# A gated mixture kept in SBUF between the attention blocks and the output blocks of two layers, with its row loads issued by ScalarE

## The reference

```python
# layer 0 (_even_mixer, branch), for latent and context rows
gate = jax.nn.silu(p[..., o_kv:])
return (jnp.concatenate([conv, attn], axis=-1) * gate) @ w_out
# layer 1 (_odd_mixer, branch), for latent rows
return (attn * jax.nn.silu(p[..., o_v:])) @ w_out
# after each layer
x = _post_norm(x, gate[:, None, :] * y, ln_g[layer], ln_b[layer])
```

## Time and profile before

| | |
|---|---|
| median of 3 runs | 4097.86 us (4092.61 to 4101.16) |
| the profiled execution, its own time | 4095.32 us |
| its span in the profile | 4093.6 us |
| PE busy | 3785.0 us, 92% of the span |
| DVE, ACT, POOL busy | 35%, 16%, 14% |
| mean granted TensorE clock | 0.975 of full speed |
| last `att_a_` product ends, first `out_a_` product starts | 1142.90 and 1182.55 us |
| last `att_c_` product ends, first `out_c_` product starts | 1830.87 and 1858.49 us |

### The profile page before, as it was taken

How to read it: one execution, slowest core, us unless ns; L and a number is a source line. 1 busy time by engine, 2 the same in 40 slices (tenths; PEclk the granted TensorE clock), 3 DMA queues, 4 the chain that set the end, 5 groups by cost and what they waited for, 6 DMA issues and landing times. The chain is left out here.

```text
span 4093.6 us, 59155 instructions
## 1 busy us (share of the span) xinstructions
PE 3785.0 (92%) x24989; PEld 1899.2 (46%) x24989; DVE 1423.6 (35%) x2623; ACT 652.7 (16%) x1339; POOL 593.2 (14%) x868
## 2 busy tenths in 40 slices
PE   8899997899979999988999999898998888888998
PEld 1354443334534444544444444453446666664443
DVE  0499983332322214222100013344534333331411
ACT  0100001122211000321110000143432222221000
POOL 0011011120100001110000011342103232322100
PEclk9899998999989999999999999999999999999999
DMA  8788996882265456436555478537773333334663
GB/s 291 293 293 288 333 358 211 297 304 81 92 249 174 165 185 228 133 122 228 182 166 172 152 288 299 202 114 246 269 240 105 111 107 118 103 101 153 222 220 103
DMA packets 360949, 818.39 MB, mean 200 GB/s; under 512 B 27922, under 2 KB 63786, under 8 KB 352994
## 3 DMA queue, kind: packets, MB, share of 16 engines
q1 hardware_dynamic: 257424, 472.27, 34.4%
q0 software_dynamic: 75008, 284.12, 19.3%
q10 hardware_dynamic: 28256, 58.26, 3.8%
HBM read 695.86 MB, written 118.70 MB: 199 GB/s over the span
## 5 line engine op out<-in xcount | busy, mean ns | idle before, releaser
L1135 PE MATMUL gemm_a_g_ps<-store_w,turned 128*128 128x512 f32 (+1 forms) x1152 | 454.8, 557 | 2.4 <-PEq L205 2.4
L1135 PE MATMUL out_c_g_ps<-store_w,turned 128*128 128x512 f32 (+1 forms) x1024 | 399.3, 553 | 0.0
L839 DVE SCALAR_TENSOR_TENSOR pmods_acc<-pmods_w,cond,pmods_acc 128x512 f32<-128x512 f32 x540 | 384.4, 749 | 24.7 <-issue 1.3
L1135 PEld LDWEIGHTS gemm_a_g_ps<-store_w,turned 128*128 128x128 f32 x1152 | 208.6, 190 | 248.1 <-issue 248.1
L2410 PE MATMUL scan_g_ps<-store_w,turned 64*64 64x512 f32 x2048 | 291.8, 607 | 10.4 <-DVE outlet_stage L2424 4.7
L1135 PEld LDWEIGHTS out_c_g_ps<-store_w,turned 128*128 128x128 f32 x1024 | 184.6, 190 | 213.7 <-issue 213.7
L1135 PE MATMUL att_a_g_ps<-store_w,turned 128*128 128x512 f32 x512 | 240.2, 600 | 6.6 <-ACT outlet_stage L2182 3.9
L1135 PE MATMUL out_a_g_ps<-store_w,turned 128*128 128x512 f32 x512 | 222.4, 597 | 1.1 <-PEq L205 1.1
L1135 PE MATMUL gemm_hq_g_ps<-store_w,turned 128*128 128x512 f32 x512 | 220.0, 592 | 1.7 <-DVEq L3230 1.7
L1135 PE MATMUL out_a_g_ps<-store_w,turned_c 128*128 128x512 f32 x512 | 220.2, 592 | 0.0
L1135 PE MATMUL feat_g_ps<-store_w,turned 128*128 128x512 f32 x384 | 179.9, 618 | 11.7 <-ACT outlet_stage L1761 9.6
(11 more groups left out here) (447 smaller groups left out, 4941.9 us busy)
## 6 DMA issues: line engine op xcount, KB each, us to landing
store_w<-in_w_in SPq DMA_DIRECT2D x160, 1024.0 KB, 5.5
pmods_w<-in_w_mod POOLq DMA_DIRECT2D x40, 2048.0 KB, 11.7
store_w<-in_a_w_in SPq DMA_DIRECT2D x48, 1024.0 KB, 9.4
store_w<-in_c_w_in SPq DMA_DIRECT2D x48, 1024.0 KB, 5.2
mods_w<-in_w_mod SPq DMA_DIRECT2D x32, 1024.0 KB, 9.3
store_w<-in_a_w_out SPq DMA_DIRECT2D x32, 1024.0 KB, 5.0
scan_raw<-s_feat SPq DMA_DIRECT2D x112, 256.0 KB, 4.6
s_feat<-feat_o POOLq DMA_DIRECT2D x16, 1536.0 KB, 7.8
```

The lines of the kernel that those rows point to most:

```text
L839: v.scalar_tensor_tensor(a, src, x, a, ALU.mult, ALU.add)
L1135: mm = pe.matmul(to, lhs, self.store.slot[i % self.store.NS][:, k, :width], start=first, stop=last)
```

## The change

- `rows_t`, a tile of 128 x 4 x 2048 float32, lives in SBUF from `att_a_` to the end of `out_c_`. The scaled attention results go straight into it; `ost` and its stores are gone. POOL loads the convolution into its first 1024 columns, four loads of 512 KB behind `load(0)`, before `late_program`.
- ACT evicts a gate tile to `outlet.stage` and stores nothing; DVE multiplies it into `rows_t` (`gate(t)`) at least six units after the tile's last product, in the order of the tiles, and after the attention units that write there. ACT's copy of tile t waits for gate t - 4. The gates are placed in `dve_order`, which also takes `rows.take` out of DVE's first program and puts it at the `rowturn`.
- ACT issues row loads 0 and 1 at the start of its list and row load j + 2 behind the eviction of job j; POOL issues the last one only. `part` is now a view of `rows_t`, and `late_program` is the plain `PartialMods` program, then the turned rows, then row load 11. `PartialMods` has two accumulators in place of four.
- The blocks `mix_a_` and `mix_c_` are gone. `out_norm_project` begins with `mixed` 0 and 1: 16 transposes of a row tile of `rows_t` on PE, one 128x512 copy for each of four banks, two by DVE and two by ACT. In `out_a_` `mixed` 2 and 3 stand behind jobs 0 and 1. `z` is `rows_t`, so POOL's load of x into a tile waits for that tile's transposes. DVE makes the gates behind `mixed` 0 and 1.

```diff
@@ ModRows
-        self.part = [st.enter_context(nc.sbuf_tensor(f"{name}_part{s}", [P, D], F32)) for s in range(2)]
+        self.part = part
@@ out_norm_project
-        z = [sb(f"z{n}", [P, D]) for n in range(4)]
+        z = [rows_t[:, n, :] for n in range(4)]
...
+        order += [("mixed", 0), ("mixed", 1)]
         if rms:
...
-            for n in range(4):
-                job(n)
+            job(0)
+            order.append(("mixed", 2))
+            job(1)
+            order.append(("mixed", 3))
+            job(2)
+            job(3)
...
+            def mixed_(tb):
+                for b in (0, 2):
+                    v.wait_ge(turned, n_turned("mixed", tb) + b + 1)
+                    last = v.tensor_copy(mixed_to(b, tb), bank_tiles(b))
+                last.then_inc(dve_done, 1)
...
-            make_gates()
             for item in order:
-                if item[0] == "sum":
+                if item == order[2]:
+                    make_gates()
+                if item[0] == "mixed":
+                    mixed_(item[1])
+                elif item[0] == "sum":
...
+                if tb in mixed_tiles:
+                    pool.wait_ge(turned, n_turned("mixed", tb) + 4)
                 pool.dma_start(zt(tb)[:, :], x_src(tb)).then_inc(x_loaded[tb], 16)
@@ attend_and_project
+                if (last is None or ("value", last) in dve_order) and done >= g.finished_by(t) + 6 and t == ripe[0]:
+                    dve_order.append(("gate", t))
+                    ripe.remove(t)
+        dve_order += [("gate", t) for t in ripe]
...
+            def gate(t):
+                n, j = g.tiles[t]
+                tb = projections[n][1][j]
+                if plan.last_unit(n, tb) is None:
+                    v.wait_ge(conv_loaded, 64)
+                v.wait_ge(copied, t + 1)
+                v.drain()
+                a = rows_t[:, tb, n * NCH:(n + 1) * NCH]
+                v.tensor_tensor(a, a, outlet.stage[t % 4][:, :], ALU.mult).then_inc(gated, 1)
...
+                if plan.gated:
+                    if t == 0:
+                        outlet.wait_stored(act, out_of)
+                    if t >= 4:
+                        act.wait_ge(gated, t - 3)
+                    g.wait_tile(act, t)
+                    act.activation(outlet.stage[t % 4][:, :], g.out(t), func).then_inc(copied, 1)
+                    return
...
+            if rows:
+                rows.load(act, 0)
+                rows.load(act, 1)
...
                     rows.evict(act, item[1])
+                    if item[1] + 2 < len(rows.jobs) - 1:
+                        rows.load(act, item[1] + 2)
...
             load(0)
+            if conv_src:
+                for tb in ALL4:
+                    pool.dma_start(rows_t[:, tb, 0:W], conv_src(tb)).then_inc(conv_loaded, 16)
@@ build, rope_and_mods
-                rows.load(pool, 0)
-                rows.load(pool, 1)
                 rope_gpsimd(pool)
...
             def late_program(pool):
-                for j in range(2, len(rows.jobs) - 1):
-                    rows.load(pool, j)
-                    mods_side.load(pool, 3 + 2 * (j - 1))
+                mods_side.gpsimd_program(pool)
                 rows.load_rows(pool)
-                mods_side.gpsimd_program(pool)
                 rows.load(pool, len(rows.jobs) - 1)
@@ build
-        turn(nc, "mix_a", ident, [(tb, [(rows(mix_a, tb), prow(proj_a, tb)[:, A_GATE:A_END])]) for tb in ALL4], D, xt(512), outlet=outlet)
...
-        turn(nc, "mix_c", ident, [(tb, [(rows(mix_c, tb), rows(proj_c, tb)[:, C_GATE:C_END])]) for tb in LAT], D, xc, outlet=outlet)
```

More of the change, by code:

```diff
@@ L1301, in out_norm_project @@
                 job(n)
-        parts = {"mul": ("pe",), "sum": ("dve",), "copy": ("act",), "norm": ("dve",), "rms": ("dve",), "turn": ("dve", "act")}
+        parts = {"mul": ("pe",), "sum": ("dve",), "copy": ("act",), "norm": ("dve",), "rms": ("dve",), "turn": ("dve", "act"), "mixed": ("dve", "act")}
         place, count = {}, {"pe": 0, "dve": 0, "act": 0}
@@ L1461, in rms_, with mixed_ @@
                 act.activation(s[:, 20:21], s[:, 19:20], ACT.Sqrt).then_inc(rooted, 1)
+            def mixed_(tb):
+                for b in (1, 3):
+                    act.wait_ge(turned, n_turned("mixed", tb) + b + 1)
+                    last = act.activation(mixed_to(b, tb), bank_tiles(b), ACT.Copy)
+                last.then_inc(act_done, 1)
             def turn(tb):
@@ L2033, in attend_and_project @@
                 act_order.append(item)
+        dve_order, done, ripe = [], 0, []
+        for item in order:
+            if item[0] == "unit":
+                done += 1
+                ripe += [t for t in range(len(g.tiles)) if plan.gated and g.finished_by(t) == done]
+            elif item[0] in ("turn", "score", "value", "rowturn"):
+                dve_order.append(item)
+            for t in list(ripe):
+                n, j = g.tiles[t]
+                last = plan.last_unit(n, projections[n][1][j])
+                if (last is None or ("value", last) in dve_order) and done >= g.finished_by(t) + 6 and t == ripe[0]:
+                    dve_order.append(("gate", t))
+                    ripe.remove(t)
+        dve_order += [("gate", t) for t in ripe]
         def wait_consumed(eng, item):
@@ L2129, in turn @@
                 v.wait_ge(filled, m + 1)
-                for dst, rows, cols in turns[n][i].targets:
-                    last = v.tensor_scalar(dst, tp[m % 2][rows, cols], turns[n][i].factor, None, ALU.mult)
+                for dst, at, cols in turns[n][i].targets:
+                    last = v.tensor_scalar(dst, tp[m % 2][at, cols], turns[n][i].factor, None, ALU.mult)
                 last.then_inc(turn_copied, 1)
@@ L2148, in scale_ @@
                 v.wait_ge(exped, u + 1)
-                if u >= 4:
+                if u >= 4 and not plan.gated:
                     v.wait_ge(out_stored[u % 4], 16 * (u // 4))
@@ L2161, in _ @@
                     scale_(item[1])
+                elif item[0] == "gate":
+                    gate(item[1])
+                elif item[0] == "rowturn":
+                    rows.take(v)
         @block.scalar
@@ L2235, in _ @@
                     mask(n + plan.slots - 1)
-            for s in range(4):
-                pool.wait_ge(out_stored[s], 16 * ((len(units) + 3 - s) // 4))
+            if not plan.gated:
+                for s in range(4):
+                    pool.wait_ge(out_stored[s], 16 * ((len(units) + 3 - s) // 4))
 class Turn:
@@ L3493, in build @@
         layer_c.close()
+        rows_layer.close()
         if upto < 4:
```

126 lines of the change are left out of this document (76 added, 50 removed).

## The result

| | before | changed |
|---|---|---|
| median of the runs taken together | 4097.69 us (4092.61 to 4101.16, 4 runs) | 4030.28 us (4017.95 to 4034.90, 4 runs) |
| ratio of the times, 95% interval | | 0.983 (0.9809 to 0.9851) |
| profiled execution, own time and span | 4095.32 and 4093.6 us | 4031.42 and 4029.6 us |
| mean granted TensorE clock | 0.975 | 0.983 |
| last `att_a_` to first `out_a_` product | 39.65 us | 1123.01 to 1132.36: 9.35 us |

The changed kernel is 67.4 us faster; I had said 59. The interval of the ratio, 4019.6 to 4036.8 us, reaches well into the range but not up to 4039: that more was won than my 59 us is clear, by how much the range was missed is not. The case I had called full clock and no delays (69 us, 4029 us), with a chance of 0.11, was nearest.

A forecast was written before the change was run, and what follows sets the result against it. PE, busy 92% of the span, was taken as the bound, so time is won where it stands still. 18.5 + 25.1 + 16.9 - 1.5 = 59.0 us off 4097.9 gave 4039 us, range 4029 to 4055.

The forecast's parts named there:

- full clock and no delays: Rival: both gaps and the first products of both output blocks at full clock; 69 us gained, 4029 us; chance 0.11.
- The block ends: After att_a_ and att_c_: last copy, last gate and block end with clear_semaphores, 0.88 us, then out_a_ and out_c_ start.
- ACT's issues hold PE back ahead of `mixed` 1: Start of out_a_: ACT issues five vector loads first, 2.5 us, so at full clock its first copy ends at 3.2 us.
- The two further groups of transposes: In out_a_, mixed 2 and 3 add 2 x 1.75 us on PE at full clock, 3.5 us.
- the clock in the gaps: Both gaps near low clock: 8.6 and 8.4 us to first product, so 28.6 us won in layer 0, 16.9 in layer 1.
- The cold first products are there before and after.: First products of out_a_ run cold, about 2 us, both before and after the change, so no difference counted.
- The row loads: In att_a_, row loads on ACT remove PE waits of 14.91 and 2.20 us and 1.4 us of slow instructions: 18.5 us.
- The moved DVE work: Gates between score and value work in the attention loops cost 0 to 10 us; 1.5 us taken.
- the cover of the sums: In att_a_, sums end at 886.2, tile 8 needs copies at 909.6: over 20 us of room, so cost nothing.
- DMA gives the wait back: Rival: late row loads or weight pieces leave 3 to 10 of the 18.5 us, 4047 to 4054 us; chance 0.20.
- The bound that decided: DMA engines busy only 0.47 of the time from 790 to 810, so the full 18.5 us was taken.
- Slower than before: Rival: row loads leave only behind evictions; slower if a load takes over 26 us, 4111 us at 30; chance 0.01.

The follow-up runs named there:

- after: First profiled execution of the changed kernel, all parts of the change against the kernel before: 4031.42 us.
- after_again: The changed kernel measured and traced again without any edit: median 4036.12 us, ratio 0.9838 to the kernel before.
- sums_late: Changed kernel plus 70 scratch clearings on DVE ahead of the first gate of att_a_, so the gates come later: 4062.46 us, one execution.
- dram_as_before: Changed kernel with its DRAM tensors laid out as before (mix_a 2048 columns wide, mix_c allocated but unused): 4028.86 us, one execution.
- rows_act: Kernel before with only the row loads moved to ACT, the last one staying on POOL; mixture still through DRAM: 4075.44 us, ratio 0.9938.
- before: First profiled execution of the kernel before the change: 4095.32 us.
- before_third: The kernel before, unedited, traced a third time: 4093.48 us, one execution.
- before_again: The kernel before, unedited, traced a second time: 4099.96 us, one execution.
- rows_pool: Changed kernel with all row loads back on POOL between the weight pieces: 4053.87 us, ratio 0.9888 to the kernel before.
- vec_late: Changed kernel with ACT issuing the output blocks' vector loads behind its copies for mixed 0 and 1, not ahead: 4034.22 us, ratio 0.9833 to before.
- two_banks: As vec_late, with mixed 1 also transposed into the empty product banks so it waits for no copy: 4024.38 us, ratio 0.983 to before.

## Why the prediction was too cautious

**Right in kind.** The gain came where it was put, without a new wait of PE on a DMA, on `store_w` or on x. The block ends came as computed: out_a_'s transposes started 2.54 us behind the last product against 2.4 forecast, out_c_'s 2.33 against 2.33. ACT's issues hold PE back ahead of `mixed` 1, as forecast: it waits 2.04 and 1.32 us at full clock, where the copy alone takes 0.78. My sum for full clock in both groups had 6.8 and 6.0 us from the block's start to the first product; measured are 6.8 and 6.1. The two further groups of transposes cost 3.5 us, and nothing stalls around them: from the first product on, `out_a_` takes 450.2 us against 446.7 in the trace of before whose first products ran at full clock.

**The step that failed: the clock in the gaps.** I took 8.6 and 8.4 us from the block's start to the first product, near the end where both groups of transposes run at the low clock (3.67 us each), because the earlier trace rows had the clock at 0.62 after 2.6 us of idle. In the changed kernel it is 6.8 us (`after`, layer 0) and 6.1 (layer 1), and 6.9 in `after_again`, layer 1, where the clock was low. Two things were wrong. First, a mean of 0.62 over 2.9 us does not say how long the low level lasts. The same trace of the kernel before, cut at the clock's own steps (window, length, busy us and instructions, granted clock, DMA share, GB/s):

```profile
773.10:773.80 0.70, 0.63 (x2) 0.99 1.01 287
773.80:777.20 3.40, 3.40 (x6) 0.50 1.02 370
777.20:780.00 2.80, 2.80 (x7) 1.00 1.05 413
```

The first product begins at 773.17 at the full clock, the low level comes 0.6 us later and is over 4 us behind that first product. It was no reason to slow the second group, which starts 4 us behind the first; 3.67 us in the earlier trace rows was measured behind 16 us of idle. Second, one row was taken for the rule. In the traces with the short gaps there are 18 places with 2.3 to 2.5 us of idle ahead of the transposes. In 10 of them the clock was low somewhere up to the first product, in 8 of these only in the first group; the other two are layer 0 of `sums_late` (2.74 and 3.65 us) and of `dram_as_before` (2.39 us in the second group alone). So the gap of layer 0 won 30.1 us instead of 28.6 and that of layer 1 18.6 instead of 16.9: 3.2 us of the 9 that were missing.

**"The cold first products are there before and after."** They are not. In 3 of 6 places in the three traces of before, job 0 begins at a clock of 0.50 and takes 2.1 us more (29.77 against 27.70 us). In both traces of the changed kernel all four began at 1.00. On the mean of these few traces that is 1.4 us in `out_a_` (+2.1 where I had +3.5) and 0.7 in `out_c_`: 2.1 us. This term is a mean over chances, and one more trace would move it: `dram_as_before` had its first job at 30.13 us.

**The row loads: 19.9 us instead of 18.5.** The waits went as forecast. `rows_act` gives 20 too. The 1.4 us beyond are not assigned to a row of the profile; part may be the clock at the start of `att_a_`: the first 32 instructions took 15.67 us in `before`, `before_third` and `after_again`, but 13.97 in `before_again`, `after` and `rows_act`.

**The moved DVE work: 0 instead of 1.5 us in `att_a_`.** `att_a_` is as long with the gates (349.0, 350.8) as without them (349.7), and `att_c_` is 0.6 us shorter. The 0 is a balance. In PE's waits those for the softmax copies fell from 5.2 to 3.7 us, in the same three places; those for the copies of the gate tiles grew from 3.9 to 4.6 us, and those for DVE ahead of eight groups of transposes from 3.2 to 4.0 us (longest 1.2 instead of 0.4). Another 0.2 us lie in the idle time ahead of `att_c_` (2.65 us in `before`, 2.1 in the other traces). The sum is then 19.9 + 30.1 - 2.1 + 0.8 + 18.6 + 0.7 = 68.0 where I had 59.0.

**Right by luck: the cover of the sums.** I wrote over 20 us and took the cost as nothing. The cost was nothing, but with 5.9 us of cover, because the sums end 11 us later than in the earlier trace rows. Counted from the block's first product to the last partial sum it took 112.5 to 113.8 us in the three traces of before, 120.1 with only the row loads on ACT (`rows_act`), 117.2 with everything but them (`rows_pool`), and 123.3 and 125.4 in the changed kernel (118.9 to 125.1 in the kernels made from it that leave this stage alone). So, one trace each, some 7 us belong to the row loads on ACT and 4 to the rest, the convolution loads among it. I had allowed 5 to 10 us for this and then set it against a cover counted from 886.2 to 909.6, which leaves out the copies behind the gate and the lateness itself: from 886.2 it was 11.1 + 5.9 = 17 us. Six more us on POOL's queue or in DVE's sums would have met PE.

**The rivals.** That DMA gives the wait back did not happen: from 830 to 890 the DMA engines are at 1.01 to 1.03, and no row is late. What came later were the partial sums, which waited for weight pieces, and they stood under cover. The bound that decided was the one I had read (0.47 around the wait). The trace does not give the landing of a single load on ACT's queue; that all came in time agrees with what the Trainium skill, "DMA: Bandwidth & Descriptors", section "Queues, rings and completion order", says of queues taking turns. `rows_pool` is no test of it: there load 2 is late because POOL issues it at 818.62 instead of 792.57. Slower than before would have needed 26 us per load; less than 14.8 is shown for load 2, and no later one made PE wait.

**The range.** Its lower end came from one part of one rival. With terms whose clock I could not tell, the whole of the full-clock case (down to 4025) belonged into it.

**Left open.** What decides whether the clock falls around an idle time between 2 and 3 us; whether ACT's issues cost what `vec_late` was to win back; whether `two_banks` is faster than the changed kernel by more than its timeline's 2 to 3 us; what lies behind the different lengths of `scan_`.

## What to carry to other kernels

If a block hands a result to the next through DRAM, price the hand-over from the last product to the next first one, and ask what is still serial when it is gone; here 39.4 and 27.4 us became 9.3 and 8.8. A load that waits in a queue behind work it does not need can be moved to the engine whose own step frees its buffer: 20 us for moving 11 issues. Ask then what those loads slow down: here the partial sums, by some 7 us. A clock that is averaged over a window must be cut at its steps before it is used for what comes later. Count cover from the last thing that has to happen, copies behind the moved step included, and shift its start by what the change itself delays, or a cost of nothing rests on luck.

## What the runs showed of the hardware

- After idle times of PE of 5.9, 13.6 and 16 to 17.6 us at the borders around the mixture the granted clock was 0.50 in every trace (1.2 GHz), and 16 transposes took 3.65 to 3.68 us instead of 1.94. After 2.3 to 2.5 us ahead of the transposes it was low in 10 of 18 places, mostly for a few us, and after 1.7 to 1.9 us (`out_c_` to the next block) in none of 13. The same kernel gave both levels in the same place: 1.94 us in `after`, 3.28 us in `after_again`.
- The length of the idle time does not decide alone. From `out_a_` to `att_c_`, after 2.1 to 2.7 us, the granted clock of the next 3 us was 0.50 to 0.68 in 13 of 14 traces; at the start of the first product of `feat_`, after 2.1 to 2.4 us, it was 1.00 in all 14. Behind the start of `att_a_` (2.6 to 3.0 us) it was low in 9 of 14.
- Slow transposes cost less than their own 1.3 to 1.6 us if PE would have waited for a copy anyway: the layer-1 gap was 8.4 us with full clock (3 traces) and 9.2 to 9.5 with a slow first group (6 traces).
- `scan_`, a stretch of 16096 matmul instructions that no kernel here changes, took 673.4 to 679.2 us in four traces without the in-SBUF mixture and 675.9 to 683.4 us in ten with it. Two single traces tell nothing under some 10 us behind such a stretch.
